# Decay sums repeated on 128 partitions by DMA instead of TensorE, and the rows' work at the two feed-forward blocks in another order

## The reference, cut to what matters

```
lower = jnp.tril(jnp.ones((q, q), dtype=bool))[None, :, :, None, None]

def step(state, inp):
    xc, ac, bc, cc = inp
    acs = jnp.cumsum(ac, axis=1)
    seg = acs[:, :, None] - acs[:, None, :]
    decay = jnp.exp(jnp.where(lower, seg, -jnp.inf))
    cb = jnp.einsum('bign,bjgn->bijg', cc, bc)
    y_diag = jnp.einsum('bijg,bijgr,bjgrp->bigrp', cb, decay, xc)
    ...
```

```
def _rms_norm(x, w):
    xf = x.astype(jnp.float32)
    y = xf * lax.rsqrt(jnp.mean(xf * xf, axis=-1, keepdims=True) + EPS)
    return (y * w.astype(jnp.float32)).astype(x.dtype)

def _swiglu(h, w1, w3, w2):
    return (jax.nn.silu(h @ w1) * (h @ w3)) @ w2
```

## Time and profile before

| | us |
|---|---|
| three runs | 2451.48, 2459.67, 2458.35 |
| median of the runs | 2458.35 |
| the profiled execution | 2453.99 |
| its span in the trace | 2452.6 |
| PE busy in it | 2379.8 |
| DVE busy | 1586.6 |
| ACT busy | 1134.8 |

### The profile page before, as it was taken

The page is one execution under the profiler, slowest core; times in us unless marked ns, Lnnn a source line. Parts: engine busy times, 40 slices in busy tenths (PEclk is TensorE's granted clock), DMA queues, the critical chain, the costliest instruction groups (busy, mean ns, idle before and its releaser), DMA issues.

```text
span 2452.6 us, 34034 instructions
## 1 busy us (share of the span) xinstructions
PE 2379.8 (97%) x13716; PEld 1913.7 (78%) x13716; DVE 1586.6 (65%) x2352; ACT 1134.8 (46%) x1690; POOL 357.8 (15%) x324
## 2 busy tenths in 40 slices
PE   6999999999899999999999989999999999999999
PEld 3876868677777877777666678989988777889988
DVE  2676676868645667655555677667753677667666
ACT  2424434343445446655555574434353546534433
POOL 0010111202232311111111110100032000201110
PEclk9999999999999999999999999999999999999999
DMA  7315234242346369999999934767542111567763
GB/s 273 116 60 182 93 126 145 87 140 96 129 154 221 119 218 384 424 423 423 423 422 423 373 130 133 168 163 185 113 144 77 44 43 52 155 147 180 174 156 109
DMA packets 127043, 467.83 MB, mean 191 GB/s; under 512 B 17194, under 2 KB 27690, under 8 KB 101153
## 3 DMA queue, kind: packets, MB, share of 16 engines
q1 hardware_dynamic: 91488, 377.42, 41.5%
q0 software_dynamic: 21952, 63.01, 12.2%
q10 hardware_dynamic: 13440, 25.17, 2.8%
HBM read 440.96 MB, written 31.72 MB: 193 GB/s over the span
## 4 chain that ended last, share of the span: by engine, by line
PE 75%; DMA 10%; DVE 8%; ACT 5%; issue 1%; SPq 0%; POOL 0%; ACTq 0%; DVEq 0%; POOLq 0%
PE bank L851 13%; PE bank L853 13%; PE bank L852 13%; DMA pair<-in_ed 8%; PE bank L1617 5%; PE bank L1619 5%; PE bank L1620 5%; PE bank L1443 2%; DVE HLB L513 2%; PE bank L1421 1%; PE bank L1423 1%; PE bank L1422 1%; ACT HLB L502 1%; PE bank L1493 1%; DVE HLB L306 1%
## 5 line engine op out<-in xcount | busy, mean ns | idle before, releaser
L513 DVE TENSOR_TENSOR HLB<-raw,HLB 128x1024 fp32r<-128x1024 f32 (+2 forms) x210 | 250.9, 1198 | 193.0 <-ACT HLB L502 192.3
L851 PE MATMUL bank<-HTh,HLB 128*128 128x512 f32 (+2 forms) x750 | 306.8, 409 | 14.8 <-DVE HLB L513 11.3
L853 PE MATMUL bank<-HTh,HLB 128*128 128x512 f32 (+2 forms) x750 | 291.6, 389 | 0.0
L852 PE MATMUL bank<-HTl,HLB 128*128 128x512 f32 (+2 forms) x750 | 290.7, 388 | 0.0
L502 ACT ACTIVATE HLB<-raw 128x1024 fp32r<-128x1024 f32 (+2 forms) x218 | 209.5, 968 | 121.2 <-PE bank L853 68.4
L502 ACT ACTIVATE HLB<-quad 128x1024 fp32r<-128x1024 f32 x133 | 139.0, 1056 | 146.0 <-PE bank L853 76.2
L513 DVE TENSOR_TENSOR HLB<-quad,HLB 128x1024 fp32r<-128x1024 f32 x133 | 161.2, 1220 | 61.4 <-ACT HLB L502 61.1
L851 PEld LDWEIGHTS bank<-HTh,HLB 128*128 128x128 f32 (+1 forms) x750 | 143.7, 192 | 72.4 <-issue 27.4
L1617 PE MATMUL bank<-HTh,HLB 128*128 128x256 f32 x608 | 170.0, 280 | 0.2 <-ACT tmp L2464 0.2
L1619 PE MATMUL bank<-HTl,HLB 128*128 128x256 f32 x608 | 169.8, 279 | 0.0
L1620 PE MATMUL bank<-HTh,HLB 128*128 128x256 f32 x608 | 169.7, 279 | 0.0
(11 more groups left out here) (671 smaller groups left out, 5902.2 us busy)
## 6 DMA issues: line engine op xcount, KB each, us to landing
quad<-in_q SPq DMA_DIRECT2D x76, 512.0 KB, 5.5
pair<-in_ed SPq DMA_DIRECT2D x32, 1024.0 KB
ht_pair<-in_eu SPq DMA_DIRECT2D x31, 1024.0 KB, 24.0
quad<-in_q POOLq DMA_DIRECT2D x57, 512.0 KB, 6.8
raw<-in_wada SPq DMA_DIRECT2D x40, 512.0 KB, 4.0
raw<-in_f SPq DMA_DIRECT2D x48, 384.0 KB, 3.4
raw<-in_eg SPq DMA_DIRECT2D x17, 1024.0 KB, 7.2
pair<-in_eu SPq DMA_DIRECT2D x17, 1024.0 KB
```

Source lines behind the costliest of these rows:

```text
L513: self.nc.vector.tensor_tensor(lo, raw, hi.bitcast(F32), ALU.subtract).then_inc(*self.w_lo.next(n))
L851: mm(bank, ah, bh, start=(start and i == 0), stop=False)
L852: mm(bank, ah, bl, start=False, stop=False)
L853: ins = mm(bank, al, bh, start=False, stop=(stop and i == n - 1))
```

## The change

It has two parts.

**The scan.** The matmuls that repeat a row are gone, and so are the one-hot columns, the low half of `ats`, and the two PSUM banks of each head. Instead ACT copies the 64 rows to SBUF once and stores them to a new tensor in the device's memory, `a_scratch` (64 x 512). Each row is then loaded onto 128 partitions, 256 KB, by a DMA that ACT issues. The forward row of head h goes straight into the tile `E4[h % 2][1]` that DVE rewrites in place; it is issued behind the exponential of head h - 2. The backward row goes into `ats`, of which there is one; it is issued behind the four subtractions of the head before. ACT and DVE subtract from SBUF instead of PSUM.

**The rows' work.** In n1 ACT copies four rows, the first weight tile's half, then the other four rows and the next; DVE makes low halves first and its sums behind them. In n2 the scaled row of each chunk and the row copies are put one chunk later.

```diff
@@ -619,8 +623,7 @@
         tw = place("tw", [128, 4, 64])
         etot = place("etot", [128, 4, 64])
         cw = place("cw", [128, 2, 64])
-        ats = place("ats", [128, 512], FR)
-        oneh = place("oneh", [128, 64, 1], FR)
+        ats = place("ats", [128, 512])
         DEC_END = at[0]
         W0 = at[0]
         XT = place("XT", [128, 8, 512])
...
@@ -1004,17 +1007,6 @@
         ORDER = [[("b", 16 + g), ("c", 20 + g)] + [("x", 4 * g + j) for j in range(4)] for g in range(4)]
         PLACE = {xc: n % 3 for n, xc in enumerate(xc for order in ORDER for _kind, xc in order)}
 
-        def pe_decayed(g, h):
-
-            for d in range(2):
-                hh = 32 * d + 8 * g + h
-                bank = psum.take(pe, ("sums", g, h, d))
-                pe.wait_ge(*dve_out.when("ats"))
-                pe.wait_ge(*act_out.when("oneh"))
-                mm(bank[:, :], oneh[:, hh, :].to_broadcast([128, 128]), ats[:, :], start=True, stop=True).then_inc(
-                    *pe_out.next(("sums", g, h, d)))
-                psum.give(("sums", g, h, d), act_out if d else dve_out, ("seg", g, h, d))
-
         AFTER = [(1, 2, 2), (1, 2, 2), (1, 2, 1), (1, 2, 1)]
 
         def pe_scan(gap):
...
@@ -1127,14 +1119,10 @@
                                 *pe_out.next(("up", g, step, d)))
                         for d in range(2):
                             psum.give(("up", g, step, d), dve_out, ("state", g, step + 1, d))
-                    else:
-                        pe_decayed(g, 0)
                     for d in range(2):
                         psum.give(("off", g, step, d), dve_out, ("tq", g, step, d))
                     gap(1, True)
                 for h in range(8):
-                    if h < 7:
-                        pe_decayed(g, h + 1)
                     if h:
                         psum.give(("yd", g, h - 1), dve_out, ("yd", g, h - 1))
                     gap(1, True)
...
@@ -1967,6 +1955,26 @@
                 yield
             store(3)
 
+        def decayed_row(g, h, d):
+            hh = 32 * d + 8 * g + h
+            return AD[hh:hh + 1, :].to_broadcast([128, 512])
+
+        def act_forward(g, h):
+
+            if h == 0:
+                act.wait_ge(*pe_out.when(("state", g, 1)))
+            elif h == 1:
+                act.wait_ge(*pe_out.when(("up", g, 2, 1)))
+            else:
+                act.wait_ge(*dve_out.when(("seg", g, h - 2)))
+            nc.scalar.dma_start(E4[h % 2][1][:, :], decayed_row(g, h, 0)).then_inc(*forward_in[h % 2].next((g, h)))
+
+        def act_backward(g, h):
+
+            if h or g:
+                act.wait_ge(*act_out.when(("seg", *((g, h - 1) if h else (g - 1, 7)), 1)))
+            nc.scalar.dma_start(ats[:, :], decayed_row(g, h, 1)).then_inc(*backward_in.next((g, h)))
+
         def act_decayed(g, h):
 
             if h == 0:
...
@@ -1975,16 +1983,20 @@
                 act.wait_ge(*pe_out.when(("up", g, 2, 1)))
             else:
                 act.wait_ge(*pe_out.when(("yd", g, h - 2)))
-            act.wait_ge(*pe_out.when(("sums", g, h, 1)))
+            act.wait_ge(*backward_in.when((g, h)))
             hh = 32 + 8 * g + h
             for c in range(4):
-                ins = activation(E4[h % 2][0][:, cols(c)], psum[("sums", g, h, 1)][:, cols(c)], ACT.Identity, scale=-1.0,
+                ins = activation(E4[h % 2][0][:, cols(c)], ats[:, cols(c)], ACT.Identity, scale=-1.0,
                                  bias=src[:, c, hh:hh + 1])
             ins.then_inc(*act_out.next(("seg", g, h, 1)))
+            if h < 7:
+                act_backward(g, h + 1)
 
         def act_exponential(g, h):
             act.wait_ge(*dve_out.when(("seg", g, h)))
             activation(E4[h % 2][0][:, :], E4[h % 2][0][:, :], ACT.Exp, scale=-1.0).then_inc(*act_out.next(("dec", g, h)))
+            if h < 6:
+                act_forward(g, h + 2)
 
         def act_start():
             s = KM["sel"]
...
@@ -2049,11 +2061,9 @@
             gap(1)
             act.wait_ge(*pe_out.when("ats"))
             act.wait_ge(*consts_in.when("pr"))
-            activation(ats[:, :], psum["ats"][:, :], ACT.Copy).then_inc(*act_out.next("ats"))
-            for i in range(2):
-                p = slice(64 * i, 64 * i + 64)
-                activation(oneh[p, :, 0], km[p, KM["ident"] + 64 * i:KM["ident"] + 64 * i + 64], ACT.Copy).then_inc(
-                    *act_out.next("oneh"))
+            activation(ats[0:64, :], psum["ats"][0:64, :], ACT.Copy).then_inc(*act_out.next("ats"))
+            act.wait_ge(*act_out.now())
+            nc.scalar.dma_start(AD, ats[0:64, :]).then_inc(*sums_out.next("rows"))
 
             def place_chunk(g, kind, xc):
                 if kind == "c":
...
@@ -2107,9 +2117,14 @@
                     act.wait_ge(*pe_out.when(("state", g, d)))
                     activation(ST[d][:, :], psum[("state", g, d)][:, :], ACT.Copy).then_inc(
                         *act_out.next(("state", g, d)))
+                if g == 0:
+                    act.wait_ge(*sums_out.when("rows"))
+                act_forward(g, 0)
+                act_backward(g, 0)
                 for step in range(4):
                     if step == 3:
                         act_decayed(g, 0)
+                        act_forward(g, 1)
                         gap(1, True, lambda: act_exponential(g, 0))
                     else:
                         gap(1, True)
...
@@ -2480,10 +2495,12 @@
 
         def act_ffn(name, w1, w3, w2, q, after):
             last = 2 * PLAIN[q] - 1
-            if name == "n1":
-                act_rows(name, range(8))
             for f in range(last + 1):
+                if name == "n1" and f == 0:
+                    act_rows(name, range(4))
                 ring.hi(act, w1, f)
+                if name == "n1" and f == 0:
+                    act_rows(name, range(4, 8))
                 ring.hi(act, w3, f)
                 if f == 0:
                     act_rms(name, ("gr", 3) if name == "n2" else None)
...
@@ -2636,8 +2653,11 @@
             act.wait_ge(*dve_out.when(("mx", 7)))
             for c in range(8):
                 ring.hi(act, "wo2", c)
-                act_scaled("n2", c, ("wo2", c))
-                act_rows("n2", range(max(c - 1, 0), 8 if c == 7 else c))
+                if c:
+                    act_scaled("n2", c - 1, ("wo2", c - 1))
+                act_rows("n2", range(max(c - 2, 0), max(c - 1, 0)))
+            act_scaled("n2", 7, ("wo2", 7))
+            act_rows("n2", (6, 7))
 
 
 
...
@@ -2732,15 +2752,9 @@
 
         def dve_decayed(g, h):
             hh = 8 * g + h
-            if h == 0:
-                dve.wait_ge(*pe_out.when(("state", g, 1)))
-            elif h == 1:
-                dve.wait_ge(*pe_out.when(("up", g, 2, 1)))
-            else:
-                dve.wait_ge(*dve_out.when(("seg", g, h - 2)))
-            dve.wait_ge(*pe_out.when(("sums", g, h, 0)))
+            dve.wait_ge(*forward_in[h % 2].when((g, h)))
             for c in range(4):
-                ins = tensor_scalar(E4[h % 2][1][:, cols(c)], psum[("sums", g, h, 0)][:, cols(c)],
+                ins = tensor_scalar(E4[h % 2][1][:, cols(c)], E4[h % 2][1][:, cols(c)],
                                     src[:, c, hh:hh + 1], -1.0, ALU.subtract, ALU.mult)
             ins.then_inc(*dve_out.next(("seg", g, h, 0)))
             dve.wait_ge(*dve_out.now())
...
@@ -2802,8 +2816,6 @@
             dve.wait_ge(*act_out.when("eacs"))
             tensor_tensor(cw[:, :, :], cw[:, :, :], dec[:, 4:6, :], ALU.mult).then_inc(*dve_out.next("co"))
             gap(1)
-            dve.wait_ge(*act_out.when("ats"))
-            rest(ats[64:128, :], psum["ats"][64:128, :], ats[64:128, :], "ats")
 
             def place_chunk(g, kind, xc):
                 if g:
...
@@ -3546,11 +3558,13 @@
 
         def dve_ffn(name, w1, w3, w2, q, after):
             last = 2 * PLAIN[q] - 1
-            if name == "n1":
-                dve_sums(name, 0, 3, 1, 2)
             for f in range(last + 1):
                 ring.lo(dve, w1, f)
+                if name == "n1" and f == 0:
+                    dve_sums(name, 0)
                 ring.lo(dve, w3, f)
+                if name == "n1" and f == 0:
+                    dve_sums(name, 3, 1, 2)
                 t = GATE[f % 2]
                 dve.wait_ge(*act_out.when(("rs", name)))
                 dve.wait_ge(*pe_out.when((w1, 0, f)))
...
@@ -3778,10 +3792,11 @@
                 dve.wait_ge(*pe_out.when(("wo2", c)))
                 tensor_tensor(XT[:, c, :], psum[("wo2", c)][:, :], XT[:, c, :], ALU.add).then_inc(
                     *dve_out.next(("wo2", c)))
-                if c:
-                    dve_scaled("n2", c - 1)
-                if c == 5:
+                if c > 1:
+                    dve_scaled("n2", c - 2)
+                if c == 6:
                     dve_sums("n2", 0)
+            dve_scaled("n2", 6)
             dve_scaled("n2", 7)
             dve_sums("n2", 3, 1, 2)
 
```

(1 more changed line is left out.)

5 lines of the change are left out of this document (4 added, 1 removed).

## The result

The changed kernel takes 2469.21 us in the median of nine runs (2465.92 to 2476.14), the one before 2453.85 in nine of its own (2448.86 to 2459.67). The ratio is **1.0066, 95% interval 1.0056 to 1.0076**: slower by some 16 us. The profiled execution has a span of 2467.9 us, against 2452.6.

The account below looks back on a forecast made before the run. PE, 97% busy, was taken as the main bound, with ACT, DVE and weight loads close behind or last in places. Scan +3, n1 0, n2 -1.8 gave +1.2 us, about +0.7 on the 2458.35 median: 2459.0 us, range 2443 to 2473.

Parts of the forecast that it names:

- rival (a): Scan: rows make weight rounds land 1.3 us later, 1.0 reaching PE in each of twelve; +11 us, 2469, chance 0.28.
- What goes, 17 us of PE: Scan: removing 32 pairs of row-repeating matmuls, 0.52 to 0.57 us each on the chain, takes away say 17 us.
- (b): Scan: ACT's issues cost the chain little, so half of PE's time is won; -11 us, 2447, chance 0.18.
- (c): Scan, n1 and n2: all of PE's time and the stalls are won; -24 us, 2434, chance 0.09.
- The middle of the argument: Scan heads: PE's gain nearly all becomes waiting for DVE; between 5 us won and 2 lost in each of four groups.
- ACT and DVE's cycle of 9.5 to 10.0 us: Scan, two heads: 9.13 us plus two row issues of 0.78 to 0.90 together, less what DVE may win from SBUF.
- The backward row's round, 4.1 to 5.1 us: Scan, each head: subtractions 1.15, issue to landing 2.9 to 3.9, some 0.1; can just tie with PE's 4.9 us.
- The sharing with the weights: Scan: one or two rows inside a weight burst delay its landing by 0.6 to 1.3 us; say +4 in all.
- The clock: Scan: a new PE wait in a burst may bring one more stretch of slow granted clock, +1 us.
- The fourth group, +2, for the issues: Scan's last group, paced by ACT and DVE: seven row issues of 0.39 to 0.45 us lengthen it, say +2.
- n1, 0, by the snapshot: n1's beginning: the 3.71 us stall goes, but PE waits 3.9 us later behind ACT's snapshot; net -1.4 to +2, 0.
- n2, -1.8: n2's beginning: moving scaling and row work one chunk later removes PE's 1.69 us stall; -1.8 us, bounds 0 and -3.

Follow-up runs that it names:

- loads of 16 partitions: Changed kernel with each row load writing 16 partitions instead of 128, an eighth of the packets, results not the reference's: 2447.00 us, 0.9974 of before.
- two buffers: Changed kernel with a second buffer for the backward row, each loaded two heads ahead, same bytes and issues: 2458.76 us, 1.0026 of the kernel before.
- An eighth of the bytes: Changed kernel loading 64 of each row's 512 columns, same transfers and packets, results not the reference's: 2462.11 us, 1.0035 of the kernel before.
- n2 alone: Kernel before with only n2's row work in the new order: 2450.32 us, 0.9993 of the kernel before.
- the kernel with only the reordered blocks: Kernel before, its scan kept, with only the row work of n1 and n2 reordered: 2448.29 us, 0.9982 of the kernel before.

## Why the prediction was right or wrong

The time, 2469.2 us, lies in the range of 2443 to 2473, but near its end. The forecast, no change within 7.4 us (0.45), didn't come; what came is **rival (a), "the rows delay the weights"** (0.28, 2469). That both numbers fit so well is in part luck. They were counted from a median of 2458.35 over three runs, and nine runs have 2453.85. Rival (a) was a loss of 11 us and the range ended at one of 15, while the measured loss is 15 to 16: counted from 2453.85, the range would have ended at 2468.5, just short of it. Point by point:

- *What goes, 17 us of PE.* PE's busy time fell by 9.4 us, and not by 15 to 20 as the text said it would. The pairs are gone. That the other 8 us are matmuls at half the clock behind the new waits is argued, not measured by itself: PE's waits of 2 us or more among the heads rose from three to eight. The granted clock, 0.990 over the span before and 0.988 after, fits: an estimate from the two is 25 and 30 us of clock lost, so some 5 more.
- *The signs.* The text expected heads of 4.7 to 5.0 us with small waits. Where PE doesn't wait, a head takes 4.4 us in the changed kernel (197.87 to 202.25), which stood as a sign of (b) or (c); but beside them stand heads of 6 to 11 us, and ACT waits for the backward row at 16 of 32 heads.
- *The middle of the argument: PE's gain goes into a wait for DVE.* Right, and shown nearly without the side effects by the loads of 16 partitions: some 2 us are won, where the working had between 5 won and 2 lost.
- *ACT and DVE's cycle of 9.5 to 10.0 us.* The terms shifted. DVE reads SBUF in less time than PSUM, four pieces in 0.87 and not 1.12 us; ACT in more, 1.29 and not 1.15. The text had nothing for ACT. An issue of a row costs 0.33 us and not the 0.39 to 0.45 that it took from the transfers of the earlier trace rows. With two buffers and all 64 issues the fourth group, where this cycle sets the pace, takes 33.1 us over its heads against 33.3 before, so the cycle didn't get longer there:

```profile
L2757 DVE TENSOR_SCALAR tmp<-tmp,src 128x128 f32<-128x128 f32 x26 | 5.7, 280 | 0.0
...
L1989 ACT ACTIVATE tmp<-ats,src 128x128 f32<-128x128 f32 x28 | 8.9, 389 | 9.1 <-DMA ats<-a_scratch 9.0
```

- *The backward row's round, 4.1 to 5.1 us.* **This step failed.** It put in 2.9 to 3.9 us from issue to landing, and a tie with PE. In the first group these were 5.2, 4.6, 6.2, 3.7 and 6.5, so the round was 5.1 to 8.2 us against a head of 4.9. It was priced as the stores of this size in the kernel before (3.9 us), and the row loads of this stretch took 4.9 in the median. The second buffer shows that the round cost some 10 us, nearly all of it from the second group on.
- *The sharing with the weights, +0.6 to +1.3 us a round, +4 in all.* **The mechanism was right and the size wrong.** The first of three weight tiles issued at 197.47 before landed after 3.6 us, and the one issued at 196.25 after the change after 6.7, +3.1. The term was worked out as bytes over 400 GB/s. An eighth of the bytes changed the weights' landing by next to nothing, an eighth of the packets brought it nearly back. With two buffers the scan still loses 11 us, and this delay is what its trace shows for them. The rule of the Trainium skill cited there (DMA: Bandwidth & Descriptors, "Issuing engines are not separate DMA queues"), that ACT's transfers and SyncE's run on the same 16 engines and interleave, agrees with these landings; the amount that the text set beside it, 1.3 us, was too small.
- *The clock.* Put at +1, for one more such wait in the scan; there were five more. What that cost by itself wasn't measured; by PE's busy time above it is 8 us at most.
- *The fourth group, +2, for the issues.* Its last head starts 4.1 us later against the third group's last one than before (16.8 us late against 12.7). But that is the single buffer, and not the issues: with two buffers it isn't later at all.
- *n1, 0, by the snapshot.* Right, in place and in size: the wait of 3.71 us at 1469.47 became one of 3.51 before the matmuls that the snapshot releases, with the half clock behind it. Reading the snapshot's wait of 0.25 us as "tied" was what gave it.
- *n2, -1.8.* In sign and place right; the traces have -2.6, the runs of n2 alone -1.7.
- *The base.* As said above: 2458.35 from three runs, 2453.85 from nine, and the profiled execution, 2453.99, was near the latter.

The table has the start of the last head's matmul (L1145, then L1133) of each group in us, and the lag against the kernel before. Its first row is the load of a weight tile (in_wz) ahead of the first group's heads, so it shows how far the kernels lay apart before any of this began:

| group | before | after | lag | two buffers | lag | 16 partitions | lag |
|---|---|---|---|---|---|---|---|
| ahead | 170.87 | 170.58 | -0.3 | 169.78 | -1.1 | 169.00 | -1.9 |
| 0 | 239.76 | 248.58 | 8.8 | 247.23 | 7.5 | 238.14 | -1.6 |
| 1 | 383.08 | 395.87 | 12.8 | 392.43 | 9.4 | 380.74 | -2.3 |
| 2 | 525.54 | 538.23 | 12.7 | 534.16 | 8.6 | 520.13 | -5.4 |
| 3 | 658.08 | 674.86 | 16.8 | 665.26 | 7.2 | 653.88 | -4.2 |

More than half of the loss is made in the first group, where weights come three at a time beside rows; the second adds 4.0 us, the third nothing, and the fourth, where ACT and DVE set the pace, 4.1. With two buffers the first group costs nearly as much, the second 1.9, and the last two nothing. Differences of 3 us between single traces mean little: the kernel with only the reordered blocks, whose scan is that of before, takes 483.9 us from the first row of this table to the last, and the kernel before 487.2.

## What to carry to other kernels

An engine at 97% isn't the bound of every stretch: before work is taken off it, read what the head's matmul would wait for next, and price the cycle of the others. A transfer that repeats a row on 128 partitions is not priced by its bytes beside other traffic: look at its packets, and at what is issued at the same moment. A row with one buffer pays its whole round on the path. And a fix in one place shows what stands behind it: in the first group the second buffer took the row off the chain, and the weights held the group nearly as long. Where an engine further on waited for PE by only 0.25 us, a stall taken away ahead of it comes back there.

## What the runs showed of the hardware

- 32 KB in 128 packets of 256 bytes landed in 4.5 us beside weight loads, and 32 KB in 16 packets of 2 KB in 2.4; 256 KB in 128 packets took 4.9.
- A block of 128 rows in one piece was cheaper than one row repeated 128 times, with the same bytes and packets: 14 us over 64 loads. Eight copies of the row, each repeated 16 times, were dearer than either: they took ACT 0.58 us instead of 0.33 to issue, and moved 200 GB/s with the DMA engines half busy. What in the chip makes the difference is open.
- The first of three weight tiles landed after 6.3 to 6.7 us where a repeated row was issued within 0.15 us of it, and after 3.6 to 3.9 where the nearest came 0.6 us behind or 1.6 us ahead.
- A 128 x 128 subtraction from SBUF instead of PSUM took DVE 280 ns and not 341, and ACT 389 and not 368.
